# Eleven expert tiles for thirteen in a hybrid encoder layer: free blocks with register-addressed weights

## The chip, the core and the metric

The kernel runs on one core of a Trainium2 chip. The metric is device microseconds of one execution, the median of several runs. The profile shows one further execution; its stretches are named by microseconds from its first instruction. TensorE, VectorE, ScalarE, GpSimd and SyncE appear in it as PE, DVE, ACT, POOL and SP, and PEld is TensorE's load of stationary weights.

## What is computed

One layer for 512 tokens of width 1024, all float32: a latent attention and a neighbourhood attention side by side, an output projection, and then a mixture of experts, which is where the change lies. Cut to that part:

```python
p_g = softmax(h @ w_rg + b_rg); g_idx = top_k(p_g, 1)            # one of 4 groups
p_e = softmax(le[of that group]); e_idx = top_k(p_e, 2)           # two of its 4 experts
combine = one_hot(4 * g_idx + e_idx) * weights                    # (512, 16)
a, u = h @ w_gate[e], h @ w_up[e]                                 # 1024 -> 256, 16 experts
out = x + sum_e (silu(a) * u * combine[e]) @ w_down[e]            # 256 -> 1024
```

Each token goes to two of 16 experts, so there are 1024 rows to compute. With the kernel's numbering of the experts (places 0 to 15) the router gives on these inputs 46, 64, 53, 69, 48, 87, 59, 36, 44, 165, 62, 35, 56, 90, 76 and 34 rows to them.

## The kernel before

**Tiles and blocks.** The expert stage works in tiles of 128 rows, each of four blocks of 32 rows. A block has one expert: `gate_up(g)` (L1669) runs 8 k-steps of four 512-column products, one per block, each against its own expert's weights (the trace shows every float32 product as two, 64 in all); `hid_turns` (L1690) transposes the hidden rows; `down(g)` (L1696) shows as 32 products. `loads_of(g)` (L332) says which expert each block has. It is a table fixed when the kernel is built: every expert has 96 places (`CAP`), 16 experts fill 12 tiles, and one further tile, the thirteenth (g = 12, `LAST`), is given to the first expert that has more than 96 rows (its number is read from a register by SP alone, `expert`, L415). Only if more were needed would `passes` (L345) run further tiles, one after another. With the counts above one is enough: expert 9 has 69 rows beyond 96.

**How rows get there and back.** DVE works out a slot for each row (`ranks_out`, L1086). POOL scatters rows into a buffer in HBM, `slot_rows`, with indirect transfers, two per 128 tokens (`dispatch`, L604, `send`, L596). Rows beyond an expert's own places wait for the counts: PE sums them (`counted`, L1651), DVE works out the further tile (`extras_out`, L1211) and the slots (`slots_out`, L1232), and POOL sends them (`overflow`, L626). Each tile's rows come back to SBUF (`load_x` on ACT's queue, L861; the first three from SP), are transposed by PE (`x_turns`, L1657) and scaled by DVE (`x_read`, L1247). The result is scaled into one of two buffers `y_sb`, left half by ACT (`left_y`, L876), right half by DVE (`right_y`, L1272), and POOL adds it to the output with an indirect accumulating transfer (`add`, L634, issued at L638). Before `add(g)` POOL waits for `add(g - 2)` (`added`, L643); the thirteenth waits for the one before too.

**Order on the queues.** SP loads expert weights, 2048 KB gate and up (`load_gu`, L405) and 1024 KB down (`load_dn`, L409), into rings of six buffers each. Load n may start when the last tile that uses load n - 6 is through (L472 to L480). The wait stands in SP's program, so all that SP issues later stands behind it. On PE the order of the steady loop (L1722 to L1730) is: `gate_up(g)`, `down(g - 1)`, `x_turns(g + 2)`, `hid_turns(g)`. On DVE it is `hidden(g)`, `right_y(g - 1)`, `x_read(g + 2)`, `tile_tags(g + 2)`, `hidden_read(g)`.

The parts that set the order are these:

```python
for g in range(ITEMS):            # POOL, L649
    if g >= 2:
        added(g - 2)
    add(g)
    if g < 2:
        overflow(2 * g)
        overflow(2 * g + 1)
```

Of the kernel before, what the change touches and what calls it, by code (L numbers as in the profile page):

```python
# [6 lines left out]
P = 128  # L7
# [37 lines left out]
CAP, BLK = 96, 32  # L45
ITEMS = E * CAP // P
EARLY = P // BLK
EXTRA = EARLY + (TOP * SEQ - EARLY * (CAP - BLK + 1)) // (CAP + 1)
FAR = 1 << 20
RING = 6  # L50
# [8 lines left out]
NK = K_FLOOR + E  # L59

# [7 lines left out]
def build(nc, x, x_turned, cols_d, rows_d, rope_d, rpb_d, consts_d, w_in_lat, w_in_k, w_in_q, w_in_v, w_qb, w_kvb, w_out, w_r,  # L68
# [8 lines left out]
    with ctx:  # L77
# [56 lines left out]
        konst = at(89, NK)  # L134

        w_gu = [at(kb, KD, 2 * F) for kb in (16, 48, 120, 32, 64, 0)]
        w_dn = [at(kb, 2, D_MODEL) for kb in (80, 171, 195, 179, 187, 136)]
# [8 lines left out]
        x_end, x_start, x_tmp, x_adj = (at(92.5 + i / 16, E) for i in range(4))  # L146
        x_hit = at(153, EXTRA, E)
        tag_sb = at(153.75, TILES, 2)
        tag_row = at(153.9375, TILES, 1).bitcast(i32)
        x_prod = at(154.0625, T, TOP, E)  # L150
# [34 lines left out]
        x_expert = sm(EXTRA).bitcast(i32)  # L185
        counts = sm(E)
# [56 lines left out]
        s_wgu = [sem(f"w_gate_up_in{r}") for r in range(RING)]  # L243
        s_wdn = [sem(f"w_down_in{r}") for r in range(RING)]
# [4 lines left out]
        s_add = [sem(f"y{r}_added_to_out") for r in range(2)]  # L249
        s_wts, s_tag = sem("row_tags_ready"), sem("tile_tags_ready")  # L250
# [64 lines left out]

        LAST = ITEMS

        turned = [("h", 0)]
        for g in range(1, LAST + 1):
            turned += [("x", i, b) for i in ((1, 2, 3) if g == 1 else (g + 2,) if g + 2 <= LAST else ()) for b in range(2)]  # L320
            turned += [("h", g)]
# [10 lines left out]
        def loads_of(g):  # L332

            if g < 3:
                return ([0, 1, 2, 3], [0, 0, 1, 1], [2, 2, 3, 3])[g]
            return [(4 * g + b) // 3 if g < ITEMS else E + g - ITEMS for b in range(4)]

        def last_item(n):
            return max(g for g in range(TILES) if n in loads_of(g))

        def added_before(g):

            return 16 * (g // 2)
# [29 lines left out]
        def _(sp):  # L373
# [31 lines left out]
            def load_gu(n, e):  # L405
                sp.dma_start(w_gu[n % RING].rearrange("p (q k) f -> p q (k f)", q=4),
                             row(w_gu_d, e)).then_inc(s_wgu[n % RING], 16)

            def load_dn(n, e):  # L409
                sp.dma_start(w_dn[n % RING], row(w_dn_d, e)).then_inc(s_wdn[n % RING], 16)  # L410
# [4 lines left out]
            def expert(n):  # L415

                if n < E:
                    return n
# [75 lines left out]
            for g in range(LAST - 1, LAST + 1):  # L494
                sp.wait_ge(s_add[g % 2], added_before(g) + 16)

        @block.gpsimd
        def _(pool):
# [132 lines left out]

            pool.wait_ge(s_out, 16 * T)

            def add(g):  # L634
# [3 lines left out]
                nc.gpsimd.indirect_dma_start(  # L638
                    out=out_rows, out_offset=bass.IndirectOffsetOnAxis(ap=tag_row[:, g, 0:1], axis=0),
                    in_=y_sb[g % 2], in_offset=None,  # L640
                    bounds_check=SEQ - 1, oob_is_err=False, compute_op=ALU.add).then_inc(s_add[g % 2], 16)

            def added(g):  # L643

                pool.wait_ge(s_add[g % 2], added_before(g) + 16)

            for g in range(ITEMS):  # L649
                if g >= 2:  # L650
                    added(g - 2)
                add(g)
                if g < 2:
                    overflow(2 * g)
                    overflow(2 * g + 1)
            added(LAST - 2)
            added(LAST - 1)
            add(LAST)

            def extra_pool(g):  # L660
                added(g - 1)
# [6 lines left out]
        def _(act):  # L668
# [215 lines left out]
            for g in range(LAST + 1):  # L884
# [3 lines left out]
                if g == 0:  # L888
                    act.wait_ge(s_disp[1], 16 * TOP * 2)
                    load_x(3)  # L890
                if g + 4 <= LAST:
                    if g + 4 == LAST:
                        act.wait_ge(s_over, 16 * TOP * T)
                    load_x(g + 4)
                if 0 < g < LAST:
                    left_y(g - 1)
# [9 lines left out]
        def _(dve):  # L906
# [179 lines left out]
            def ranks_out(t):  # L1086
# [9 lines left out]
                nc.vector.tensor_scalar(over, KB_OF[t][:, 32:32 + E], CAP - 0.5, float(FAR), ALU.is_gt, ALU.mult).then_inc(s_cnt, 1)  # L1096
                dve.wait_ge(s_cnt, t + 1)
                link(nc.vector.tensor_tensor(early, early, slot, ALU.add))
                link(nc.vector.tensor_tensor(early, early, over, ALU.add))
# [110 lines left out]
            ranks_out(T - 1)  # L1210
            def extras_out():  # L1211

                dve.wait_ge(s_countr, 1)
# [605 lines left out]
```

## Time and profile before

| what | value |
|---|---|
| runs | 500.72, 502.74, 502.3 us; median 502.3 |
| the profiled execution | 502.5 us, its span 500.6 us |
| mean granted TensorE clock | 0.981 |
| TensorE busy | 464.3 us, 93% |
| DVE, ACT, POOL busy | 44%, 30%, 31% |
| DMA | 102.66 MB, 205 GB/s over the span |

The expert stage begins at about 327 us and lasts to the end. Busy PE time holds pipelined products, so it is the intervals between equal steps that tell a tile's cost. In a row of the timeline the columns are start, length, engine, line, operation, operands, count, and in brackets the idle time ahead and what ended it. In the rows of windows the DMA share is that of 16 engines; it can come out a little over 1.

### The profile page before, as it was taken

The numbers are of one execution on the slowest core, as the hardware profiler recorded it, in microseconds if no ns is written. First come the engines' busy times: TensorE is split into PE (matmuls) and PEld (weight loads), VectorE is DVE, ScalarE is ACT, GpSimd is POOL, SyncE is SP. The second block draws the span as 40 slices with busy tenths as digits, with TensorE's granted clock in tenths as the row PEclk, the third lists the DMA queues.
The fourth block names the chain that finished last, engine by engine and source line by source line (L and its number), as shares of the span: only waits on it lengthen the run. The fifth ranks groups of instructions, "written<-read, shape, count | busy, mean of one in ns | idle before, by whom it ended". The sixth has DMA issues, their size and how long they took to land.

```text
span 500.6 us, 7676 instructions
## 1 busy us (share of the span) xinstructions
PE 464.3 (93%) x2826; PEld 226.8 (45%) x2826; DVE 220.1 (44%) x696; ACT 147.8 (30%) x340; POOL 152.9 (31%) x163
## 2 busy tenths in 40 slices
PE   5999999989999999999999998896999999998982
PEld 2544544444555565554556555632333333342320
DVE  2133855515765545454555748655222222231310
ACT  1322513325455566453343523230001011000000
POOL 1150288878299920000000202220351111111121
PEclk9999999999999999999999989879999999999997
DMA  8999960005100000094010349799599999999531
GB/s 317 386 412 363 403 264 2 1 0 209 65 2 0 1 1 1 9 404 177 0 45 1 126 169 347 288 344 354 192 356 383 389 375 403 389 374 398 171 56 26
DMA packets 28873, 102.66 MB, mean 205 GB/s; under 512 B 3744, under 2 KB 5280, under 8 KB 28448
## 3 DMA queue, kind: packets, MB, share of 16 engines
q1 hardware_dynamic: 22640, 88.25, 45.7%
q0 software_dynamic: 4176, 8.42, 7.0%
q10 hardware_dynamic: 2016, 5.46, 2.8%
q8 instruction: 25, 0.41, 0.3%
q14 instruction: 16, 0.13, 0.1%
HBM read 79.50 MB, written 29.44 MB: 218 GB/s over the span
## 4 chain that ended last, share of the span: by engine, by line
PE 72%; DVE 8%; POOL 7%; DMA 6%; issue 5%; ACT 1%; POOLq 0%; SPq 0%; DVEq 0%
PE bank L1685 17%; PE bank L1346 14%; PE bank L1516 10%; PE bank L1709 8%; PE bank L1330 6%; PE bank L1418 5%; PE bank L1435 5%; POOL small L509 3%; DMA slot_rows<-arena,small 3%; DMA arena<-slot_rows 3%; PE bank L1666 2%; PE bank L1459 2%; DVE arena L987 1%; POOL arena L365 1%; DVE arena L989 1%
## 5 line engine op out<-in xcount | busy, mean ns | idle before, releaser
L1346 PE MATMUL bank<-arena 128*128 128x512 f32 (+1 forms) x256 | 111.1, 584 | 5.4 <-DVE arena L931 5.4
L1685 PE MATMUL bank<-arena 128*32 128x512 f32 x832 | 94.1, 603 | 2.7 <-DVE arena L1269 1.8
L1346 PEld LDWEIGHTS bank<-arena 128*128 128x128 f32 x256 | 48.2, 195 | 53.5 <-issue 53.1
L1330 PEld LDWEIGHTS bank<-arena 128*128 128x128 f32 (+1 forms) x356 | 42.9, 141 | 39.3 <-issue 32.3
L638 POOL DMA_INDIRECT out<-arena x13 | 20.2, 1550 | 130.6 <-DVE arena L1276 101.4
L1330 PE MATMUL bank<-arena 128*128 128x128 f32 (+1 forms) x356 | 51.4, 277 | 5.7 <-DVE arena L994 2.8
L1516 PE MATMUL bank<-arena 128*128 128x512 f32 x112 | 55.6, 620 | 0.6 <-issue 0.6
L1685 PEld LDWEIGHTS bank<-arena 128*32 128x32 f32 x832 | 26.7, 111 | 58.7 <-issue 56.7
L1709 PE MATMUL bank<-arena 128*32 128x512 f32 x416 | 47.1, 593 | 1.0 <-DVE arena L1269 1.0
L1003 DVE COPY arena<-bank 128x512 f32<-128x512 f32 (+2 forms) x64 | 35.8, 582 | 22.2 <-PE bank L1330 22.2
L874 ACT ACTIVATE arena<-bank 128x256 f32<-128x256 f32 x13 | 5.0, 385 | 126.1 <-PE bank L1685 126.1
L513 POOL TENSOR_SCALAR small<-small 128x1 f32<-128x1 f32 x16 | 3.6, 223 | 123.6 <-DVE small L1042 71.8
L1262 DVE TENSOR_TENSOR arena<-arena,bank 128x256 f32<-128x256 f32 x13 | 5.5, 421 | 74.2 <-ACT arena L874 74.2
L728 ACT ACTIVATE arena<-arena,small 128x512 f32<-128x512 f32 (+2 forms) x64 | 34.7, 590 | 3.7 <-DVE small L1011 3.6
L509 POOL TENSOR_TENSOR small<-small 128x24 f32<-128x24 f32 (+2 forms) x7 | 29.8, 4261 | 16.3 <-DVE small L982 9.3
L1128 DVE TENSOR_REDUCE small<-bank 128x1 f32<-128x512 f32 x32 | 22.1, 692 | 28.4 <-PE bank L1418 28.3
L1418 PE MATMUL bank<-arena 96*128 96x512 f32 x64 | 34.0, 615 | 0.0
L790 ACT ACTIVATE arena<-bank,small 128x512 f32<-128x512 f32 x32 | 22.0, 688 | 34.6 <-DVE small L1128 34.5
L1435 PE MATMUL bank<-arena 128*64 128x128 f32 x416 | 29.8, 280 | 1.6 <-DVE arena L1003 1.6
L1435 PEld LDWEIGHTS bank<-arena 128*64 128x64 f32 x416 | 22.1, 136 | 16.3 <-issue 14.6
L529 POOL TENSOR_TENSOR arena<-arena 128x512 f32<-128x512 f32 (+2 forms) x20 | 22.0, 1121 | 21.5 <-issue 13.7
L1516 PEld LDWEIGHTS bank<-arena 128*128 128x128 f32 x112 | 19.5, 194 | 18.7 <-issue 18.7
(176 smaller groups left out, 500.3 us busy)
## 6 DMA issues: line engine op xcount, KB each, us to landing
arena<-in_w_gu SPq DMA_DIRECT2D x17, 2048.0 KB, 23.8
arena<-in_w_dn SPq DMA_DIRECT2D x17, 1024.0 KB, 22.7
slot_rows<-arena SPq DMA_DIRECT2D x1, 11822.0 KB, 47.7
arena<-slot_rows ACTq DMA_DIRECT2D x10, 514.0 KB
arena<-in_w_out SPq DMA_DIRECT2D x2, 2048.0 KB, 8.2
arena<-in_x_turned SPq DMA_DIRECT2D x4, 512.0 KB, 8.1
arena<-in_x SPq DMA_DIRECT2D x4, 512.0 KB, 13.3
arena<-in_w_in_k SPq DMA_DIRECT2D x1, 2048.0 KB, 14.7
```

The costliest lines, as they stand in the source:

```text
L509: nc.gpsimd.tensor_tensor(v, v, mhalf[:, 0:n], ALU.pow).then_inc(s_root, 1)
L529: nc.gpsimd.tensor_tensor(dst, src, src, ALU.mult).then_inc(s_sqr, 1)
L728: nc.scalar.activation(probs, probs, ACT.Copy, scale=rsum[:, t % 2, u // MU, h:h + 1]).then_inc(s_ps, 1)
L1003: nc.vector.tensor_copy(PT[u % 2][:, 0:blocks, :], TPB[p % 2][:, 0:blocks * P].rearrange("p (a b) -> p a b", a=blocks))\
L1128: nc.vector.tensor_reduce(nmax[:, u % 2, u % H:u % H + 1], SB[u % 2][:, :], AX.X, ALU.max, negate=True).then_inc(s_mx, 1)
L1330: last = nc.tensor.transpose(TPB[p % 2][0:s.shape[-1], b * P:(b + 1) * P], s, ident)
L1346: last = nc.tensor.matmul(product_bank(i)[:, 0:width], hT[:, t, k, :], w[:, k, :], start=(k == 0), stop=(k == KD - 1))
L1418: nc.tensor.matmul(SB[u % 2][:, :], qT[:, h, t * P:(t + 1) * P], kT[:, h, :], start=True, stop=True).then_inc(s_S, 1)
L1435: last = nc.tensor.matmul(OB[t % 2][DV * j:DV * (j + 1), pair * P:(pair + 1) * P], v[:, first + b, h * DV:(h + 1) * DV], PT[j][:, b, :], s ...
L1516: last = nc.tensor.matmul(YB[b][:, :], src[:, k, :], w_o[half][:, k, b * 512:(b + 1) * 512], start=(k == 0), stop=(k == 3))
L1685: last = nc.tensor.matmul(GU[g % 2][BLK * b:BLK * (b + 1), :], xT[g % 2][:, k, BLK * b:BLK * (b + 1)], w_gu[n % RING][:, k, :], start=(k = ...
L1709: last = nc.tensor.matmul(YR[g % 2][half][BLK * b:BLK * (b + 1), :], hidT[g % 2][:, k, BLK * b:BLK * (b + 1)], w_dn[n % RING][:, k, half * ...
```

## The change

The layout of blocks becomes a table of 11 tiles. Most experts have two blocks of their own (64 rows), experts 14 and 15 four, and in tiles 3 to 9 the first block is free: DVE gives it, from the counts, to an expert whose weights are in SBUF at that time, and PE reads their place from a register, for gate/up and for down. Further tiles run only if rows are left, from none up (`EXTRA` is 15, `slot_rows` has 26 tiles for 23). The ring of gate/up weights has seven buffers, the seventh over `h2s`, the rows that POOL scatters; so SP waits for the last overflow transfer before that load, and ACT waits for it before it loads tiles 3, 4 and 5. All eight overflow transfers are issued ahead of the first add. Each add waits for the one before, and a tile with a free block is added in two transfers, one after the other: its first 32 rows, then the 128 with the first 32 out of range. `extras_out` and `slots_out` do more, and `places_out` is new.

```diff
-CAP, BLK = 96, 32
-ITEMS = E * CAP // P
+BLK = 32
+GU_RING, DN_RING = 7, 6
+FREE = -1
+LAYOUT = [[0, 1, 2, 3], [0, 1, 2, 3], [4, 4, 5, 5], [FREE, 6, 6, 7], [FREE, 7, 8, 8], [FREE, 9, 9, 10],
+          [FREE, 10, 11, 11], [FREE, 12, 12, 13], [FREE, 13, 13, 14], [FREE, 14, 14, 14], [15, 15, 15, 15]]
+ITEMS = len(LAYOUT)
+LAST_USE = [1, 1, 1, 3, 3, 4, 5, 5, 6, 8, 9, 9, 9, 9, 9, 10]
...
+EXTRA = 15
...
+GU_KB = (16, 48, 120, 32, 64, 0, 92.875)
...
-        LAST = ITEMS
-
-        turned = [("h", 0)]
+        LAST = ITEMS - 1
+
+        def turned_in(g):
+
+            return {1: (), 2: (3, 4)}.get(g, (g + 2,) if g + 2 <= LAST else ())
...
             with ExitStack() as more:
-                for i in range(1, EXTRA):
+                for i in range(EXTRA):
...
             load_dn(5, 5)
-            for g in range(LAST):
-                for n in range(RING, E + 1):
-                    if last_item(n - RING) == g - 1:
+            sp.wait_ge(s_over, 16 * TOP * T)
+            load_gu(6, 6)
+            for g in range(ITEMS):
+                for n in range(GU_RING, E):
+                    if LAST_USE[n - GU_RING] == g:
+                        sp.wait_ge(s_gu, g + 1)
+                        load_gu(n, n)
+                for n in range(DN_RING, E):
+                    if LAST_USE[n - DN_RING] == g - 1:
                         sp.wait_ge(s_dn, 2 * g)
-                        load_dn(n, expert(n))
-                for n in range(RING, E + 1):
-                    if last_item(n - RING) == g:
-                        sp.wait_ge(s_gu, g + 1)
-                        load_gu(n, expert(n))
+                        load_dn(n, n)
...
+            for t in range(T):
+                overflow(t)
             pool.wait_ge(s_out, 16 * T)
...
+                if loads_of(g)[0] == FREE:
+                    add_rows(g, tag_row[:, g, 0:1], BLK)
+                    pool.wait_ge(s_add[g % 2], added_before(g) + 16)
+                    add_rows(g, own_row[:, g - FREE_0, 0:1], P)
+                else:
+                    add_rows(g, tag_row[:, g, 0:1], P)
+
+            for g in range(LAST):
+                if g > 0:
+                    added(g - 1)
                 add(g)
...
-            for g in range(LAST + 1):
+            silu(0)
+            left_y(0)
+            silu(1)
+            act.wait_ge(s_over, 16 * TOP * T)
+            for g in (3, 4, 5):
+                load_x(g)
+            for g in range(2, LAST + 1):
...
                 for k in steps:
                     for b, n in enumerate(loads_of(g)):
+                        if n == FREE:
+                            w = arena[:, bass.ds(free_at[g][0] + k * 2 * F, 2 * F)]
+                        else:
+                            w = w_gu[n % GU_RING][:, k, :]
...
+            def free_places(g):
+
+                if g == FREE_0:
+                    pe.wait_ge(s_free, 1)
+                i = g - FREE_0
+                free_at[g] = [pe.value_load(v[0:1, i:i + 1], min_val=0, max_val=int(max(kbs) * KB))
+                              for v, kbs in ((gu_at, GU_KB), (dn_at, DN_KB))]
```

In the cut parts, `extras_out` becomes 50 small DVE instructions for 18 up to the point where it sets `s_most`, and the four behind that move into `extra_places_out`, after the first tiles' tags; `slots_out` becomes 18 for 10, most of them of 64 elements per partition; `places_out` adds 11 after the tags of tile 2. Every free tile adds one DVE instruction to its tags.

## Rows read from the trace of the kernel before

**Rows 1.** The page: PE's busy time, and the DMA row in 40 slices of 12.5 us.

```profile
PE 464.3 (93%) x2826; PEld 226.8 (45%) x2826; DVE 220.1 (44%) x696; ACT 147.8 (30%) x340; POOL 152.9 (31%) x163
...
DMA  8999960005100000094010349799599999999531
```

**Rows 2.** Timeline of PE, expert stage.

```profile
346.49 1.09 PE L1666 MATMUL bank<-arena 128*128 128x128 f32 x8 [3.04 <-DMA arena<-slot_rows]
...
357.19 7.07 PE L1685 MATMUL bank<-arena 128*32 128x512 f32 x64
...
368.87 7.07 PE L1685 MATMUL bank<-arena 128*32 128x512 f32 x64
...
452.57 7.07 PE L1685 MATMUL bank<-arena 128*32 128x512 f32 x64 [1.76 <-DVE arena L1269]
459.43 3.64 PE L1709 MATMUL bank<-arena 128*32 128x512 f32 x32
```

**Rows 3.** Windows: length, busy us of PE, PEld, DVE, ACT, POOL, clock, DMA share, GB/s.

```profile
325.00:330.00 5.00, 4.07 (x20) 2.05 (x23) 2.67 (x22) 4.12 (x13) 1.07 (x2) 0.50 1.00 324
...
350.00:355.00 5.00, 5.00 (x52) 1.56 (x48) 0.67 (x5) 0.00 (x0) 0.00 (x0) 1.00 0.33 105
...
360.00:465.00 105.00, 103.19 (x938) 37.42 (x934) 27.81 (x77) 9.65 (x18) 20.33 (x17) 1.00 1.03 383
```

**Rows 4.** Timeline of SP's queue.

```profile
338.75 0.51 SPq L410 DMA_DIRECT2D arena<-in_w_dn  x1
355.92 0.94 SPq L406 DMA_DIRECT2D arena<-in_w_gu  x2
```

**Rows 5.** DMA queues of 380 to 400 us: packets, MB, share of 16 engines.

```profile
q1 hardware_dynamic: 1513, 5.95, 73.3%
q0 software_dynamic: 527, 0.75, 16.8%
q10 hardware_dynamic: 288, 1.05, 12.9%
```

**Rows 6.** Timeline of DVE, routing work beside tile 0.

```profile
333.06 0.60 DVE L1216 SCALAR_TENSOR_TENSOR arena<-small,arena 128x16 f32<-128x16 f32 x3
...
333.90 0.15 DVE L1220 COPY arena<-arena 128x1 f32<-128x1 f32 x1
...
334.17 0.17 DVE L1220 COPY arena<-arena 128x2 f32<-128x2 f32 x1
...
338.38 0.42 DVE L1262 TENSOR_TENSOR arena<-arena,bank 128x256 f32<-128x256 f32 x1 [1.76 <-ACT arena L874]
...
340.08 0.22 DVE L1238 TENSOR_TENSOR arena<-arena 128x64 f32<-128x64 f32 x1
```

**Rows 7.** Timeline of POOL: two overflow transfers, the add of tile 6, the last add.

```profile
361.25 0.97 POOL L598 DMA_INDIRECT slot_rows<-arena,small  x1 [0.30 <-issue]
362.52 0.97 POOL L598 DMA_INDIRECT slot_rows<-arena,small  x1 [0.30 <-issue]
...
427.83 1.53 POOL L638 DMA_INDIRECT out<-arena  x1 [10.13 <-DVE arena L1276]
...
492.89 1.54 POOL L638 DMA_INDIRECT out<-arena  x1 [9.18 <-DVE arena L1276]
```

**Rows 8.** The chain that ended last: landings of two scatters, the last add's release.

```profile
311.54 9.40 DMA slot_rows<-arena,small
...
332.43 5.44 DMA slot_rows<-arena,small
...
491.95 0.02 issue
```

**Rows 9.** The software queue in 432.3 to 436.6 us: packets, MB, share.

```profile
q0 software_dynamic: 144, 0.31, 37.0%
```

**Rows 10.** SP's last wait, for the last adds: length in ns and time.

```profile
L495 SPq EVENT_SEMAPHORE  x1: 28/28/28, 499.2 to 499.2; - x1
```

**Rows 11.** Register work of SP's one register-addressed gate/up load: length in ns.

```profile
L406 SPq FUSED_REGOPS  x1: 48/48/48, 447.9 to 447.9; - x1
```

More of the change, by code:

```diff
@@ L58 @@
 K_FLOOR = K_LOW + E
-NK = K_FLOOR + E
+K_CAP = K_FLOOR + E
+K_FROM = K_CAP + E
+K_END = K_FROM + E
+K_MOST = K_END + E
+K_GU = K_MOST + E
+K_DN = K_GU + E
+K_LEAST = K_DN + E
+K_OWN = K_LEAST + FREES
+NK = K_OWN + 1
+GU_KB = (16, 48, 120, 32, 64, 0, 92.875)
+DN_KB = (80, 171, 195, 179, 187, 136)
 TILES = ITEMS + EXTRA
@@ L637, in add @@
                 pool.wait_ge(s_tag, g + 1)
[L638 to L651, printed above, removed]
-                add(g)
[L653 to L657, printed above, removed]
+                if loads_of(g)[0] == FREE:
[7 more added lines that the diff above has]
+                    added(g - 1)
+                add(g)
             add(LAST)
             def extra_pool(g):
+                added(g - 2)
                 added(g - 1)
@@ L1210, in _, with table, running @@
             ranks_out(T - 1)
+            def table(k):
+                return konst[:, k:k + E]
+            def running(a, b, op):
+                for shift in (1, 2, 4, 8):
+                    nc.vector.tensor_copy(b[:, 0:shift], a[:, 0:shift])
+                    link(nc.vector.tensor_tensor(b[:, shift:E], a[:, shift:E], a[:, 0:E - shift], op))
+                    a, b = b, a
             def extras_out():
                 dve.wait_ge(s_countr, 1)
-                link(nc.vector.tensor_scalar(x_tmp, counts, float(CAP), None, ALU.is_gt))
@@ L1215, in extras_out @@
-                for bound in range(CAP + P, SEQ, P):
-                    link(nc.vector.scalar_tensor_tensor(x_tmp, counts, float(bound), x_tmp, ALU.is_gt, ALU.add))
-                a, b = x_start, x_end
-                link(nc.vector.tensor_copy(a, x_tmp))
-                for shift in (1, 2, 4, 8):
-                    nc.vector.tensor_copy(b[:, 0:shift], a[:, 0:shift])
-                    link(nc.vector.tensor_tensor(b[:, shift:E], a[:, shift:E], a[:, 0:E - shift], ALU.add))
-                    a, b = b, a
+                link(nc.vector.tensor_tensor(beyond, counts, table(K_CAP), ALU.subtract))
@@ new lines, in extras_out @@
+                link(nc.vector.tensor_scalar(wanted, beyond, 1.0, None, ALU.is_gt))
+                for bound in range(BLK, max(FREE_MOST) * BLK, BLK):
+                    link(nc.vector.scalar_tensor_tensor(wanted, beyond, bound + 1.0, wanted, ALU.is_gt, ALU.add))
+                link(nc.vector.tensor_tensor(wanted, wanted, table(K_MOST), ALU.min))
+                link(nc.vector.tensor_copy(sum_a, wanted))
+                running(sum_a, sum_b, ALU.add)
+                link(nc.vector.tensor_tensor(sum_a, sum_a, wanted, ALU.subtract))
@@ new lines, in extras_out @@
+                link(nc.vector.tensor_tensor(max_a, table(K_FROM), sum_a, ALU.subtract))
+                running(max_a, max_b, ALU.max)
+                link(nc.vector.tensor_tensor(f_start, max_a, sum_a, ALU.add))
+                link(nc.vector.tensor_tensor(f_blocks, table(K_END), f_start, ALU.subtract))
+                link(nc.vector.scalar_tensor_tensor(f_blocks, f_blocks, 0.0, wanted, ALU.max, ALU.min))
+                nc.vector.tensor_scalar(f_row, f_start, float(P), None, ALU.mult)
+                nc.vector.tensor_scalar(f_rows, f_blocks, float(BLK), None, ALU.mult)
@@ L1223, in extras_out @@
+                link(nc.vector.scalar_tensor_tensor(x_rows, f_blocks, -float(BLK), beyond, ALU.mult, ALU.add))
+                link(nc.vector.tensor_scalar(x_tmp, x_rows, 1.0, None, ALU.is_gt))
+                for bound in range(P, SEQ, P):
+                    link(nc.vector.scalar_tensor_tensor(x_tmp, x_rows, bound + 1.0, x_tmp, ALU.is_gt, ALU.add))
+                link(nc.vector.tensor_copy(x_start, x_tmp))
+                running(x_start, x_end, ALU.add)
                 link(nc.vector.tensor_copy(x_end, x_start))
@@ L1301, in _ @@
                 tile_tags(g)
+            places_out()
+            extra_places_out()
             for g in range(1, LAST + 1):
@@ L1307, in _ @@
                     right_y(g - 1)
-                if g + 2 <= LAST:
-                    x_read(g + 2)
-                    tile_tags(g + 2)
+                for i in turned_in(g):
+                    x_read(i)
+                    tile_tags(i)
                 hidden_read(g)
```

182 lines of the change are left out of this document (120 added, 62 removed).

## The prediction

> **What bounds the kernel now.** I read the page first: PE is busy 93% of the span, and in its last third the DMA row stands at nine tenths too [rows 1]. So two resources are near their limit in the expert stage, and taking a tile away from one of them need not move the end. The timeline of PE gives the price of a tile: gate/up of tile 2 starts at 357.19 us, that of tile 3 at 368.87, so 11.68 us, and the same from tile to tile up to the ninth [rows 2]. The one break in the pattern is ahead of tile 10, at 452.57, 1.8 us. The windows show the DMA engines full from 360 to 465 us (share 1.03, 383 GB/s), but two thirds idle just ahead of that, 0.33 in 350 to 355 us [rows 3]. The timeline of SP's queue says why: its load at 338.75 is the last that is free to go, and the next waits for tile 1's products, at 355.92 [rows 4]. So PE sets the pace and the DMA keeps up with nothing in hand.
>
> The price of each kind of transfer comes from the queues of 380 to 400 us [rows 5]. SP's queue moved 5.95 MB in 73.3% of 20 us, 406 GB/s: 5.2 us for a gate/up load of 2.1 MB, 2.6 us for a down load. ACT's queue moved two row tiles in 12.9%: 1.3 us each. Two adds took 16.8%: 1.7 us each, in occupied engine time; their delay is another matter, below.
>
> **Two tiles less.** The counts fit the new table: experts 3, 5, 9 and 13 have 5, 23, 101 and 26 rows beyond 64, which want 1, 1, 4 and 1 free blocks, seven in all, and their windows (tile 3; 3 or 4; 5 to 8; up to 9) hold them. No further tile runs. On PE alone: 2 x 11.68 = 23.4 us less, a span of 477.2.
>
> **The routing work on DVE.** The steps of 16 columns come every 0.20 us, those in pairs every 0.14 (333.90 to 334.17) [rows 6]. The new `extras_out` has 50 steps for 18, 24 of them in pairs: 26 x 0.20 + 24 x 0.14 = 8.6 us. It starts two steps ahead of 333.06 as before, so it ends near 341.4. `hidden(0)` ran at 338.38 [rows 6] and goes 3 us later, and `down(0)` with it, which so ends at about 346.3. Its cover is the wait for tile 1's rows, which PE turned at 346.49 after 3.04 us idle [rows 2]; without that cover it would cost 3 us. `slots_out` has 18 steps of 64 columns, 0.22 us long [rows 6] and 0.25 with the link between two; from 342.7 it ends at about 347. `x_read(1)` then starts near 348, 0.7 us late, which I leave in the rounding. `places_out` (11 steps, 3 us) and the longer tags lie beside tile 1's products. The larger zero fill (26 tiles for 23) and constants lie in stretches where the DMA row is 0 or 1 [rows 1]: nothing.
>
> **The load behind the overflow.** Eight overflow transfers now go together from 347.2, one each 1.27 us [rows 7], the last is issued by 357.4. From there to landing a scatter took 5.44 and 9.40 us with the engines full [rows 8]; here they are empty, so I take 4.5, with 3 and 8 as ends: 362. SP may load expert 6 only then, and ACT the rows of tiles 3 to 5. Behind SP's wait stands every later weight load, those of experts 7, 8 and 9 first, which were free since 356. Tile 3 needs 6 and 7: 2 x 5.2, with three row tiles (3.9) and an add (1.7) between them, and about 2 us until the last byte counts: 380. Tile 3 began at 368.87 before, so 11 us of the 23 go back.
>
> **Then the transfers bound it.** Until `down(7)` can run, the experts' loads up to down 13 must land: from 362 us 10 gate/up and 8 down loads (72.8 us), 8 row tiles (10.4) and 5 adds (8.5): 454. What PE still has then equals what it had in the kernel before at `down(9)`: from 459.43 to the end, 500.6, 41.2 us [rows 2]. So this limit gives a span of 495, 5.4 less than now, if the adds stay hidden.
>
> **The adds.** Here I find the new bound. The add that POOL starts at 427.83 [rows 7] has its 144 packets in 432.3 to 436.6 us [rows 9]: 8.8 us from start to landing while the queue of weights is full. The last one starts at 492.89 [rows 7] and SP sees it at 499.2 [rows 10]: 6.3 us with nothing beside it, of which 2.1 are ahead of the packets if these take the same 4.3. So far no one waits for either, since an add waits only for the one two before. Now each waits for its predecessor, and tiles 3 to 9 have two in a row. Release to start is 0.94 us (491.95 to 492.89) [rows 7, 8]. The 32-row transfer is not in the trace: its packets start as late (4.5 us full, 2.1 empty) and take between a quarter of 4.3 us and all of it, so 5.6 to 8.8 us full, 3.2 to 6.3 empty. I take 5.9 and 3.5, near the lower ends, as it has a quarter of the rows. A free tile then costs POOL 5.9 + 0.9 + 8.8 + 0.9 = 16.5 us under load and 3.5 + 0.9 + 6.3 + 0.9 = 11.6 us without, against the 11.68 of PE.
>
> The chain in order: gate/up of tile 3 at 380.5, of tile 4 at 392.2, `down(3)` ends at 402.7, its two halves are scaled at 403.5, POOL starts at 404.4. Three cycles under load put the add of tile 6 at 454, where the weights run out. Tiles 6 to 9 take 11.6 us each, with 3 us more for the last two down loads that still come: tile 10's add starts at 503, lands at 509.5, and 1.4 us later the program ends (499.2 to 500.6): 511. Behind POOL's waits stand `left_y` and `right_y`, which need the buffer back, so DVE's `right_y(g - 1)` holds `hidden_read(g)` and PE runs at most three tiles ahead; that costs nothing more as long as the adds are the slower chain.
>
> The Trainium skill, DMA: Bandwidth & Descriptors, section "Anatomy of one DMA — SWDGE (gpsimd) path", fits one such transfer as 2.0 us plus its bytes at 436 GB/s. By that rule a 128-row add would take 3.2 us and a 32-row one 2.3, and the pair with its releases 7.3 us, hidden under any tile. The row shows 6.3 us for the 128 rows, and 8.8 under load, so I go by the rows.
>
> **Registers on PE.** A quarter of a free tile's 96 products, 24, are addressed by a register. SP's one such load shows 48 ns of register work [rows 11]: 1.2 us a tile if PE's sequencer isn't ahead, some 2 with the two register loads; nothing if it is. I take nothing, since PE waits for weights or for the adds in these tiles; as upper end 7 x 2 = 14 us. After waits the granted clock was 0.50 in 325 to 330 us [rows 3], the lower of the two levels; after the gap of some 12 us ahead of tile 3 I expect the same for a few microseconds. On its own that adds 3 us to tile 3, in the upper end.
>
> **Sum.** 500.6 - 23.4 + 11 + 7 (transfers) gives the 495 of the hidden case, and + 16 from the adds gives 511. The profiled execution was 1.9 us over its span (502.5 for 500.6) and 0.2 over the median of the runs, so the time is 513 us, 2.1% over 502.3. A change of under 0.5% can hardly be told from none.
>
> **Rivals.**
> 1. *The adds stay hidden, the transfers bound it.* Place: tiles 3 to 9. It holds if a pair of adds takes under about 13 us with loads beside it. For it: fewer adds crowd the queue. Against: 8.8 us for one alone [rows 7, 9]. Time: 495 + 1.9 = 497, faster by 1%. Chance 0.20.
> 2. *PE stays the bound.* The overflow lands by 356, as the loads went before, and the free blocks don't hold weights back: 477.2 + 1.9 = 479, or up to 490 with half of the stall. Against: eight transfers can't be issued before 357, and the engines were full with six buffers. Chance 0.09.
> 3. *Registers and clock.* PE pays 2 us in each free tile and runs part of it at the lower clock, in a chain with the adds' waits: 513 + 10 to 513 + 16, so 523 to 529. Chance 0.11.
> 4. *A further tile runs after all*, serial, with its own loads: at least 20 us, 530 or more. The counts speak against it. Chance 0.03.
> The forecast has 0.57, with 505 to 521 as its own range (32-row transfer at its two ends, overflow landing 3 us either way).
>
> **How the numbers follow.** Slower by over 0.5% (above 504.8): the forecast but for 0.05 of it, and rivals 3 and 4: 0.66. Faster (below 499.8): rival 2 and 0.13 of rival 1, 0.22. The rest, 0.12, is within. The range must reach rival 1 and the lower half of rival 3: 494 to 524.
>
> **What would show it.** In the trace of the changed kernel: 11 groups of 64 gate/up products; idle PE ahead of the third of them in tile 3, to about 380 us; SP's first load after 338 at about 362; POOL's adds in tiles 3 to 9 as pairs, 15 to 17 us from pair to pair under load, back to back, with POOL waiting for DMA rather than for DVE L1276; DVE's and ACT's scaling waiting for DMA; SP's queue drained well before 470. I am wrong if POOL still waits for DVE between tiles, if PE has no gap ahead of tile 3, or if a pair takes under 12 us.

## The result, and the profile after

| kernel | median | ratio to before | span of the profiled run |
|---|---|---|---|
| before, measured beside it | 501.92 us (4 runs) | | 500.6 us |
| changed | 534.55 us (533.29 to 536.09, 4 runs) | 1.0654, interval 1.0615 to 1.0692 | 534.3 us |

The changed kernel is 6.5% slower. The prediction had the sign (slower, 0.66) but not the size: 513 with 494 to 524. What happened is the forecast's chain and rival 4 behind it: a twelfth tile ran.

In the changed kernel the products of gate/up stand at L1799, those of down at L1827, the turning of rows at L1776, the adds at L679, SP's loads at L448 and L452, the overflow's scatters at L640 and the scaling that releases an add at L1382. The page, with PE, the clock row and the DMA row in slices of 13.4 us, answers to [rows 1]:

```profile
PE 469.0 (88%) x2720; PEld 225.9 (42%) x2720; DVE 226.3 (42%) x747; ACT 146.7 (27%) x338; POOL 160.8 (30%) x169
...
PEclk9999999999999999999999895799898998999577
DMA  8999950005000000930107499919999999543810
```

PE has 106 products fewer. Two tiles would be twice 106 (`thr7` below, with both gone, has 2614), so only one tile has gone. At the end of the DMA row stands an "8" that the kernel before did not have. The timeline of PE (start, length, engine, line, operation, count, idle time ahead and what ended it) answers to [rows 2]:

```profile
379.78 8.77 PE L1799 MATMUL bank<-arena 128*32 x64 [2.50 <-DMA arena<-in_w_gu]
...
403.34 5.34 PE L1827 MATMUL bank<-arena 128*32 x32 [3.10 <-DMA arena<-in_w_dn]
...
454.71 7.07 PE L1799 MATMUL bank<-arena 128*32 x64
...
466.39 7.07 PE L1799 MATMUL bank<-arena 128*32 x64
...
489.62 3.64 PE L1827 MATMUL bank<-arena 128*32 128x512 f32 x32 [0.52 <-DVE arena L1375]
507.18 1.97 PE L1776 MATMUL bank<-arena 128*128 128x128 f32 x8 [13.92 <-DMA arena<-slot_rows]
...
509.93 8.89 PE L1799 MATMUL bank<-arena 128*32 128x512 f32 x64 [0.78 <-DVE arena L1359]
```

Tile 3 starts at 379.78, where 380 was forecast. Two neighbouring free tiles, 454.71 and 466.39, are 11.68 us apart, so products addressed by a register cost nothing. `down(10)`, the last planned step, starts at 489.62; then PE is idle for 13.92 us and a further tile begins. The timeline of SP's queue answers to [rows 4]:

```profile
338.32 0.43 SPq L452 DMA_DIRECT2D arena<-in_w_dn  x1
360.42 9.32 SPq L448 DMA_DIRECT2D arena<-in_w_gu  x4
...
494.06 0.41 SPq L448 DMA_DIRECT2D arena<-in_w_gu  x1
```

SP's first late load goes at 360.42 (forecast 362), behind the overflow. The weights and the rows of the further tile are issued only when `down(10)` is through. The chain that ended last shows the rows landing 12 us later:

```profile
495.15 11.98 DMA arena<-slot_rows
```

Last, the timeline of POOL, which answers to [rows 7]:

```profile
357.58 0.97 POOL L640 DMA_INDIRECT slot_rows<-arena,small  x1 [0.30 <-issue]
...
410.45 1.33 POOL L679 DMA_INDIRECT out<-arena  x1 [15.17 <-DVE arena L1382]
...
428.79 1.33 POOL L679 DMA_INDIRECT out<-arena  x1 [10.12 <-DMA out<-arena,small]
...
445.38 1.33 POOL L679 DMA_INDIRECT out<-arena  x1 [8.34 <-DMA out<-arena,small]
...
461.85 1.33 POOL L679 DMA_INDIRECT out<-arena  x1 [8.09 <-DMA out<-arena,small]
...
472.64 1.33 POOL L679 DMA_INDIRECT out<-arena  x1 [5.04 <-DMA out<-arena,small]
...
504.82 1.54 POOL L679 DMA_INDIRECT out<-arena,small  x1 [5.91 <-DMA out<-arena]
506.67 1.54 POOL L679 DMA_INDIRECT out<-arena  x1 [0.30 <-issue]
526.16 1.54 POOL L679 DMA_INDIRECT out<-arena  x1 [17.95 <-DVE arena L1382]
```

The last scatter starts at 357.58, near the 357.4 forecast. In tiles 4 to 9 POOL waits for DMA, not for DVE as in [rows 7], but for two adds (435.50, released by DVE, and 486.09, by ACT). From pair to pair it is 18.3, 16.6 and 16.5 us with the weights' queue full, where 16.5 was forecast, and 10.8, 13.5 and 11.5 without, where 11.6 was forecast. So nearly all of the forecast stands in this trace, and a tile behind it.

### The profile page after: what moved, and what is told of

Its sections match the earlier page's. It is cut to its first block, busy times and chain, and to the rows that moved or that the text cites. A ratio compares the mean times of both kernels' runs of the same rounds, so it can differ in the third digit from the quotient of the medians.

```text
span 534.3 us, 7638 instructions
## 1 busy us (share of the span) xinstructions
PE 469.0 (88%) x2720; PEld 225.9 (42%) x2720; DVE 226.3 (42%) x747; ACT 146.7 (27%) x338; POOL 160.8 (30%) x169
## 4 chain that ended last, share of the span: by engine, by line
PE 63%; DMA 15%; DVE 9%; POOL 6%; issue 4%; ACT 1%; SPq 0%; POOLq 0%; DVEq 0%
PE bank L1456 13%; PE bank L1799 11%; PE bank L1626 10%; DMA arena<-in_w_gu 7%; PE bank L1827 6%; PE bank L1440 5%; PE bank L1545 5%; PE bank L1528 5%; DMA arena<-in_w_dn 5%; POOL small L551 3%; DMA arena<-slot_rows 2%; PE bank L1569 2%; PE bank L1636 1%; PE bank L1652 1%; PE bank L1776 1%
## 5 line engine op out<-in xcount | busy, mean ns | idle before, releaser
L1799 PE MATMUL bank<-arena 128*32 128x512 f32 (+1 forms) x768 | 95.1, 631 | 7.1 <-DMA arena<-in_w_gu 4.6
L1456 PEld LDWEIGHTS bank<-arena 128*128 128x128 f32 x256 | 48.4, 196 | 54.2 <-issue 53.8
L1827 PE MATMUL bank<-arena 128*32 128x512 f32 (+1 forms) x384 | 48.5, 649 | 9.9 <-DMA arena<-in_w_dn 8.4
L1799 PEld LDWEIGHTS bank<-arena 128*32 128x32 f32 x768 | 25.1, 115 | 66.7 <-issue 65.4
L679 POOL DMA_INDIRECT out<-arena x12 | 17.1, 1424 | 110.4 <-DVE arena L1382 64.9
L640 POOL DMA_INDIRECT slot_rows<-arena,small x16 | 16.0, 997 | 51.7 <-DVE small L1154 32.6
L1827 PEld LDWEIGHTS bank<-arena 128*32 128x32 f32 x384 | 14.0, 118 | 41.3 <-issue 38.5
L1382 DVE TENSOR_SCALAR arena<-bank,arena 128x512 f32<-128x512 f32 x12 | 9.0, 751 | 52.9 <-PE bank L1827 38.2
```

The source lines that it names most:

```text
L1456: last = nc.tensor.matmul(product_bank(i)[:, 0:width], hT[:, t, k, :], w[:, k, :], start=(k == 0), stop=(k == KD - 1))
L1799: last = nc.tensor.matmul(GU[g % 2][BLK * b:BLK * (b + 1), :], xT[g % 2][:, k, BLK * b:BLK * (b + 1)], w, start=(k == 0), stop=(k == KD - 1))
L1827: last = nc.tensor.matmul(YR[g % 2][half][BLK * b:BLK * (b + 1), :], hidT[g % 2][:, k, BLK * b:BLK * (b + 1)], w, start=(k == 0), stop=(k ...
```

## Why a tile was left over

The expert stage places the first 256 tokens before all counts are known. So that the next tokens' rows start behind each early block, `pads` (L1141 here, L1091 before) raises the count of an expert of tile 0 to the 32 rows of its block when the first 256 tokens brought fewer. In the kernel's own order of tokens these bring 30, 26, 29 and 57 rows to experts 0 to 3 (counted from the reference's router), so 2, 6, 3 and 0 places stay empty. Expert 1 has 64 rows, which looked like an exact fit in two blocks; with six empty places it needs 70. Its weights are used last in tile 1, where no block is free. Six rows are over, and the kernel runs a whole tile for them.

The kernel before has the same pads. They cost it nothing, since 96 places hold 70.

## The experiments

The runs fall into four groups, each on one chip with the kernel before beside it (medians 502.9, 503.18, 503.42 and 503.57 us, in the order below); each ratio is within its group. The number that DVE compares to decide on a further tile is half more than the rows left, since `K_CAP` holds 32 rows per block less a half: 6.5 for six rows.

### thr6 and thr7: without the further tile

`thr6` (one run) and `thr7` raise the bound from which a further tile runs. `thr7` so leaves six of the 1024 rows uncomputed, and with them the further tile.

```diff
-                link(nc.vector.tensor_scalar(x_tmp, x_rows, 1.0, None, ALU.is_gt))
+                link(nc.vector.tensor_scalar(x_tmp, x_rows, 7.0, None, ALU.is_gt))   # thr6: 6.0
```

> The changed kernel, but a further tile is asked for only where an expert has more than 6 rows left over, instead of more than 0.5. Theory P (the padding of tile 0 pushes expert 1 to 70 places of 64, 6 rows over, and that is what calls the twelfth tile): 6.5 counts as over, the tile runs, 534 us as for the changed kernel. Rival Q (many rows are left over, because the free blocks don't reach the experts they were meant for): 534 us here as well, and again 534 with a bound of 7. Rival R (only one to five rows over): no further tile, about 514.

> The same with more than 7 rows as the bound; no further tile if 6 rows are all that is left over, and those 6 of 1024 rows stay out of the result. Theory P: the rest of the trace is unchanged, the last add starts near 506.5 and lands 6.3 us later, so a span of 514 and a time of 515 to 516, ratio 1.027 to the kernel before. Rival Q: 534 as before.

`thr6`: 535.67 us, so the tile still ran. `thr7`: 511.02 us, ratio 1.0144 (1.0102 to 1.0185), and no further tile. The compared number is over 6 and not over 7, as the 6.5 that the pads give: six rows are left, and no more. The tile costs 0.051 by the ratios, some 25 us; the spans, 534.3 and 509.8, say 24.5. `thr7` is the case that the forecast spoke of, and its time lies 2 us beside the 513; it is 4 us below the 515 to 516 expected of this run, since the last add starts at 502.55 and not near 506.5. Its chain that ended last, in order of time:

```profile
422.12 26.32 DMA arena<-in_w_dn
...
468.26 5.37 DMA out<-arena,small
...
474.43 3.59 DMA out<-arena
...
478.79 6.17 DMA out<-arena,small
...
485.75 3.30 DMA out<-arena
...
489.81 6.43 DMA out<-arena,small
...
497.04 2.90 DMA out<-arena
```

Up to 449 us it waits for weights, and from 468 on it is adds one after another, the 32 rows (2.9 to 3.6 us) and the 128 (5.4 to 6.4).

### one and lag: without the pairs, without the wait

Both stand on `thr7` and leave out the free blocks' rows: tiles 3 to 9 have one add. `lag` also waits, from tile 3 on, only for the add two before, as the kernel before does, and ahead of the last add for both that are still out.

```diff
-            return 16 * (2 if loads_of(g)[0] == FREE else 1)
+            return 16
...
-                    add_rows(g, tag_row[:, g, 0:1], BLK)
-                    pool.wait_ge(s_add[g % 2], added_before(g) + 16)
                     add_rows(g, own_row[:, g - FREE_0, 0:1], P)
...
-                    added(g - 1)
+                    added(g - (1 if g < 3 else 2))        # lag alone
...
+            added(LAST - 2)                               # lag alone
+            added(LAST - 1)                               # lag alone
```

> As the one with the bound of 7, but in tiles 3 to 9 only the second of the two adds is issued, so the rows of the free blocks are left out of the result; each add still waits for the one before. Theory A (from tile 3 on the serial pairs of adds set the end): 8 to 12 us less than with both, 503 to 507. Rival B (the weights' transfers set the end, the adds are hidden behind them): within 2 us of the one with both adds.

> As the last one, and from tile 3 on an add waits only for the one two before, as in the kernel before. Theory A: once there is one add per tile it takes 9.7 us with the release, under the tile's 11.68, so the wait costs under 2 us more; the transfers are the bound then, a time of 497 to 503. Rival C (the wait itself costs much even with one add): 5 us or more below the last one.

`one`: 503.78 us (1.0007, 0.9983 to 1.0031). `lag`: 504.25 us (1.0027, 0.9999 to 1.0054), 1 us above its expected range. So the second add of each pair costs 7.2 us (511.02 to 503.78), and waiting for the one before instead of the one two before costs nothing. And with the adds out of the way the kernel is still no faster than before, though it runs two tiles less. Why is seen in `lag`. Timeline of PE:

```profile
411.79 9.75 PE L1799 MATMUL bank<-arena 128*32 x64 [5.72 <-DMA arena<-in_w_gu]
...
449.39 6.39 PE L1827 MATMUL bank<-arena 128*32 x32 [4.22 <-DMA arena<-in_w_dn]
...
463.85 3.62 PE L1827 MATMUL bank<-arena 128*32 x32
```

The chain that ended last, between these:

```profile
361.44 18.54 DMA arena<-in_w_gu
...
388.77 22.79 DMA arena<-in_w_gu
...
425.05 24.11 DMA arena<-in_w_dn
```

And the windows (length, busy us of PE, PEld, DVE, ACT, POOL, clock, DMA share, GB/s):

```profile
405.00:425.00 20.00, 14.28 (x107) 4.28 (x106) 3.14 (x10) 1.07 (x2) 1.54 (x1) 0.83 1.02 392
...
445.00:450.00 5.00, 0.78 (x8) 0.38 (x8) 0.42 (x1) 0.38 (x1) 0.00 (x0) 0.80 1.02 382
```

From 361 to 450 us three loads stand on the chain, each landing 18 to 24 us after its release, with the engines full (share 1.02 to 1.03 in every window from 365 to 450). Over the two stretches shown, each with a wait in it, the granted clock is 0.83 and 0.80, a mix of its two levels of 1.2 and 2.4 GHz, and the steps behind the waits are longer: 9.75 us for a gate/up that else takes 7.07, 6.39 for a down that else takes 3.62.

### half and laghalf: a shorter overflow

The first 256 tokens have no row beyond their places, so the first four of the eight overflow transfers carry nothing. `half` is `thr7` without them, `laghalf` is `lag` without them.

```diff
-            sp.wait_ge(s_over, 16 * TOP * T)      # and the same on ACT
+            sp.wait_ge(s_over, 16 * TOP * 2)
...
-            for t in range(T):
+            for t in range(2, T):
                 overflow(t)
```

> As the one with the bound of 7 (both adds), but only the last four overflow transfers are issued, those of tokens 256 to 511, and SP and ACT wait for these; the first four carry no row on these inputs. Theory S (the loads behind the overflow hold up tile 3, one for one): SP's first late load at 355 instead of 360, tile 3's products 5 us earlier, and as everything behind it shifts, 4 to 6 us less in all, 505 to 507. Rival T (the order of the weights' transfers is the bound, not their start): 2 us or less.

> The same with one add per tile and the wait for the one two before. Theory S: 4 to 6 us under the 504.3 of that kernel with all eight overflow transfers, 498 to 500. Rival T: 502 or more. If nearly all of the gap of 5 us in tile 1's products goes too, the burst of transfers on POOL is what made it.

`half`: 504.62 us (1.0024, 0.9997 to 1.0051), 6.4 below `thr7`. `laghalf`: 497.86 us (0.9889, 0.9854 to 0.9924), 6.4 below `lag`. In `half`, SP's queue and then PE:

```profile
353.31 9.98 SPq L448 DMA_DIRECT2D arena<-in_w_gu  x4
```

```profile
373.38 8.77 PE L1799 MATMUL bank<-arena 128*32 x64 [3.13 <-DMA arena<-in_w_gu]
```

In `thr7` the same two steps stand at 361.27 and 380.67 us. The first late load goes 8.0 us earlier, tile 3 starts 7.3 earlier, and the medians move by 6.4, with pairs and without (6.0 and 6.9 by the ratios, as the kernels compared are of different groups). Both times lie just below their expected ranges. But the shorter overflow is not all that differs: in the traces of `thr7` and `lag` tile 1's products stall for some 5 us (last section), in those of `half` and `laghalf` they don't. In `thr7` tile 3 waits last for DVE L1375 (1.83 us), on a chain that goes back through that stall. How much of the 6.4 us is the stall's is not shown. The pair in the next experiment is free of it.

### lay and layhalf: a place for expert 1's six rows

`lay` computes all rows. It gives expert 1 a third block of its own, in tile 2, and keeps 11 tiles and seven free blocks. `layhalf` is `lay` with the four empty overflow transfers left out.

```diff
-LAYOUT = [[0, 1, 2, 3], [0, 1, 2, 3], [4, 4, 5, 5], [FREE, 6, 6, 7], [FREE, 7, 8, 8], [FREE, 9, 9, 10],
-          [FREE, 10, 11, 11], [FREE, 12, 12, 13], [FREE, 13, 13, 14], [FREE, 14, 14, 14], [15, 15, 15, 15]]
+LAYOUT = [[0, 1, 2, 3], [0, 2, 3, 1], [1, 4, 4, 4], [FREE, 5, 5, 6], [FREE, 6, 7, 7], [FREE, 8, 8, 9],
+          [FREE, 9, 10, 10], [FREE, 11, 11, 12], [FREE, 12, 13, 13], [FREE, 14, 14, 14], [15, 15, 15, 15]]
...
-LAST_USE = [1, 1, 1, 3, 3, 4, 5, 5, 6, 8, 9, 9, 9, 9, 9, 10]
+LAST_USE = [1, 2, 1, 3, 3, 4, 5, 5, 6, 8, 9, 9, 9, 9, 9, 10]
```

> The changed kernel with another table of blocks and nothing else: expert 1 gets a third block of its own (tile 1 is 0, 2, 3, 1 and tile 2 is 1, 4, 4, 4), expert 5 moves to tile 3, and all experts from 6 on move back by one or two blocks. All rows are computed. Theory P: no further tile, as 70 places fit in 96. Tile 3 needs only the weights of expert 6, not 7, so it starts at about 375 instead of 380. The pairs of adds still end last: 506 to 511. Rival Q: a further tile still runs, 530 or more.

> That table with the last four overflow transfers alone. All rows are computed on these inputs. By theory S and the table together the weights come 5 us sooner: 502 to 507, so at best level with the kernel before, as the pairs of adds remain. If it comes out under 500, the adds have slack.

`lay`: 506.54 us (1.0074, 1.0041 to 1.0107), 28 us less than the changed kernel for a change of two tables. `layhalf`: 502.32 us (0.9984, 0.996 to 1.0008). Both are within what was expected. They are of one group, and neither trace has the stall: the first late load goes at 358.83 and at 355.31, and 3.5 us there are worth 4.2 at the end (4.5 by the ratios). So with the order of the loads as it is, the expert stage has hardly any slack behind the overflow. The chain that ended last of `lay` prices the adds:

```profile
440.25 6.77 DMA out<-arena
...
447.79 9.00 DMA out<-arena,small
...
457.58 3.49 DMA out<-arena
...
461.84 6.59 DMA out<-arena,small
```

From POOL's start to landing 32 rows take 6.8 us under load and 3.4 to 3.7 without, 128 rows 9.0 and 5.7 to 6.6. The 6.8 is a high one: in the chains of `half`, `layhalf` and `order` 32 rows under load take 5.9 to 6.2 us.

### order and orderlag: loads in order of need

Both compute on `lay`'s table. Expert 6's gate and up go into the buffer that tile 1 frees, expert 7's over `h2s`, and SP issues the loads in the order in which PE needs them. `orderlag` also has one add per free tile (the free blocks' rows left out) and, from tile 4 on, waits for the one two before (in `lag` from tile 3 on).

```diff
+def place(n):
+    return {6: 0, 7: 6}.get(n, n % GU_RING)
...
-            sp.wait_ge(s_over, 16 * TOP * T)
+            sp.wait_ge(s_gu, 2)
             load_gu(6, 6)
-            for g in range(ITEMS):
...
+            sp.wait_ge(s_over, 16 * TOP * T)
+            load_gu(7, 7)
+            sp.wait_ge(s_dn, 4)
+            load_dn(6, 6)
+            sp.wait_ge(s_gu, 3)
+            load_gu(8, 8)
+            load_gu(9, 9)
+            load_dn(8, 8)
...
```

> The table with three own blocks for expert 1, and the weights of experts 6 and 7 change places: 6 goes into the buffer that tile 1 frees, 7 into the one over the scattered rows, and SP issues the loads in the order in which they are needed. All rows are computed, all eight overflow transfers and both adds are there. Theory S with A: the first late load goes at 356, no wait for weights in tile 3 or for the down load in tile 3, so the first pair of adds starts at about 395 instead of 405.5. Behind it the pairs take 16.5 us under load and 11.6 without, 91.7 us from tile 3 to tile 10 in the kernel with that table, up to 98 now as more of them run beside loads: a span of 494 to 501, a time of 496 to 503. Rival T: nothing gained over the 506.5 of the table alone.

> The same with one add in tiles 3 to 9 (the rows of the free blocks stay out of the result) and, from tile 4 on, the wait for the add two before. What the pairs of adds still cost: theory A says 5 to 12 us, so 486 to 494, with PE close to its pace of 11.68 us a tile. If it comes within 3 us of the one with the pairs, the transfers are the bound there too.

`order`: 505.39 us (1.0048, 1.002 to 1.0076), 2 us above the expected range; its interval and that of `lay` overlap, so the rival "nothing gained" is not ruled out. `orderlag`: 493.01 us (0.9827, 0.9783 to 0.9871). In `order` the rows of the next tiles arrive late, then the last step of PE:

```profile
370.01 1.09 PE L1792 MATMUL bank<-arena 128*128 128x128 f32 x8 [2.22 <-DMA arena<-slot_rows]
372.61 1.97 PE L1792 MATMUL bank<-arena 128*128 128x128 f32 x8 [1.51 <-DMA arena<-slot_rows]
...
480.38 5.34 PE L1843 MATMUL bank<-arena 128*32 128x512 f32 x32 [0.52 <-DVE arena L1391]
```

and the adds of POOL:

```profile
400.79 1.33 POOL L695 DMA_INDIRECT out<-arena  x1 [10.18 <-DVE arena L1398]
...
495.84 1.54 POOL L695 DMA_INDIRECT out<-arena  x1 [0.30 <-issue]
```

PE is through at 485.7, the last add starts ten microseconds later: here the chain of adds is the bound, 95 us from 400.79 to 495.84, and the pairs, with the wait for the add before, cost 12.4 us (505.39 to 493.01).

Why so little came of the earlier loads is in the same trace. Expert 6's load goes at 356.02, as meant, but the last overflow scatter now lands beside it. The chain that ended last has it as

```profile
355.55 7.62 DMA slot_rows<-arena,small
```

In `lay` the last scatter starts at 355.70 and ACT loads the next tiles' rows 3.1 us later; here it is 7.6 us. Tile 3 has its weights but waits for its rows and starts at 374.94, later than `lay`'s 372.13. What is gained comes behind it: `down(3)`, which waits 6.33 us for its weights in `lay`, has them here, so the first pair of adds starts at 400.79 (405.55 in `lay`, 395 expected). In `orderlag` the rows come later still:

```profile
374.44 1.97 PE L1792 MATMUL bank<-arena 128*128 128x128 f32 x8 [5.89 <-DMA arena<-slot_rows]
...
380.50 8.26 PE L1815 MATMUL bank<-arena 128*32 x64
```

### alt and layalt: a shorter chain of adds

In tiles 4, 6 and 8 the 128-row add goes first, without waiting for the one of the tile before; then come both waits and the 32 rows. The 32 rows of the next tile follow them. So of four transfers per two tiles only three stand in a row. Neighbouring tiles' adds of 128 rows are then in flight together, as they are in the kernel before, where `add(g)` waits for `add(g - 2)` alone; no more freedom than that was taken. `alt` has this on `order`, `layalt` on `lay`; both compute all rows.

```diff
-                if loads_of(g)[0] == FREE:
+                if loads_of(g)[0] == FREE and g % 2:
                     add_rows(g, tag_row[:, g, 0:1], BLK)
...
+                elif loads_of(g)[0] == FREE:
+                    add_rows(g, own_row[:, g - FREE_0, 0:1], P)
+                    added(g - 1)
+                    pool.wait_ge(s_add[g % 2], added_before(g) + 16)
+                    add_rows(g, tag_row[:, g, 0:1], BLK)
...
-                if g > 0:
+                if g in (1, 2) or g % 2:
                     added(g - 1)
```

> The last kernel with both adds, but in tiles 4, 6 and 8 the own rows go first, without a wait for the own rows of the tile before (their experts are of different groups, so no token is in both), and the free block's rows go last. Two adds of 128 rows then run side by side in every second tile, and the chain of a pair of tiles has three landings to wait for and a release in place of four: under load about 6.8 + 9.7 + 1.9 + 6.8 = 25 us for 33, so 12.6 a tile, near PE's 11.68. Theory A: of the 12.4 us that the pairs cost in that kernel 9 to 11 go, 494 to 497, faster than both kernels. If the adds' landings slow each other down by as much, 500 or more.

> The table with three own blocks for expert 1 (506.5 us), the loads in the order of the changed kernel, and the same alternating adds. Theory A: the transfers are the next bound, between tile 3's later start and the free adds, 499 to 502. If it is as low as the one with the ordered loads, that order is worth nothing.

`alt`: 499.63 us (0.9927, 0.9899 to 0.9954), `layalt`: 499.5 us (0.9946, 0.9915 to 0.9977). Both beat the kernel before, by 0.5 to 0.7% by the ratios, and the changed kernel by 35 us. That is a small gain over the kernel before, but both intervals end below 1. `layalt` is within its expected range, `alt` came out 3 us above its own. Between these two the order of the loads is worth nothing measurable. But in the profiled run of `alt` its early start was missing: SP's first late load waits for tile 1's products, these stalled (last section), and it went at 363.31 and not at 356.02 as in `order`:

```profile
363.31 0.94 SPq L454 DMA_DIRECT2D arena<-in_w_gu  x2
```

Later two down loads hold PE, until 424.44 and 454.56. How much of the 3 us is due to the stall is not shown. The timeline of POOL in `alt`:

```profile
408.66 1.54 POOL L695 DMA_INDIRECT out<-arena,small  x1 [5.41 <-DMA out<-arena]
413.47 1.54 POOL L695 DMA_INDIRECT out<-arena,small  x1 [3.27 <-issue]
423.63 1.33 POOL L695 DMA_INDIRECT out<-arena  x1 [8.63 <-DMA out<-arena,small]
```

The second 128 rows start 4.8 us after the first and don't wait for their landing. Not tried: one add for both kinds of rows. A token may stand in the free block and in an own block of the same tile, which is why the change adds them apart.

## Why the prediction was wrong, step by step

**Two tiles less: the step that failed.** "The counts fit the new table ... No further tile runs." I took the rows that the router gives and compared them with the places. The kernel compares rows and pads, and for expert 1 that is 70 against 64. Rival 4 named the outcome and got 0.03, because I took the fit of 64 in 64 for a certainty. Its price was right as a bound ("at least 20 us, 530 or more"): 24.5 us by the spans, 534.55 in all. A fit without a place to spare should have sent me to every line that changes the count.

**The routing work on DVE** ended at 347.57 (347 forecast), but its cover was thinner than I had it: `down(0)` ended at 348.55, not 346.3, and tile 1's products started at 350.63, 1.8 us later than before and not 0.7. That cost nothing by itself, as tile 3 waited for its weights all the same.

**The load behind the overflow: right in its two times.** 362 forecast, 360.42 measured; tile 3 at 380, measured 379.78. Between the last scatter's start and SP's load lie only 2.8 us; I had 4.5, with 3 as the lower end. The "about 2 us until the last byte counts" in the sum for tile 3 have no row behind them, and no run shows them apart. What four overflow transfers fewer are worth is 4.2 us by `lay` and `layhalf`; the 6.4 of `half` may have the stall in it.

**Transfers and adds: the sum right in part by luck, its split wrong.** I had 495 for the span with hidden adds, and 16 us for the adds. The runs give 502.3 (`one`) and 503.5 (`lag`), and 7.2 us. So the transfers cost 7 to 9 us more than I gave them and the adds 9 less. In the hidden case I had asked when all loads up to down 13 are in, 454 us, and let `down(7)` start there. In `lag` an earlier step binds: `down(6)` waits for its own weights until 449.39, takes 6.39 us at the lower clock and is followed by a gate/up, so `down(7)` starts at 463.85, ten later. The lower clock after a wait for weights stood in my upper end only, for tile 3 alone; on `lag`'s chain it is worth 2.7 and 2.8 us at the two steps shown above.

The chain of adds came out near 511 because errors cancel. In `thr7` the first pair starts at 411.0, not 404.4, since `down(3)` waits for weights too: 6.6 late. Three pairs under load take 53.1 us (411.00 to 464.06), not 49.5. But from there to the last add it is 38.5 us (to 502.55), not 49: the pairs without load take 10.4 to 11.3 us, the 3 us that I had added for the last loads don't show, and the last add waits for no other. I had read the loop over `range(LAST)` as if it held the last tile, but `add(LAST)` stands behind it without the wait. The changed kernel's row shows it too: 504.82 and 506.67, 0.30 us idle between them. I had 7.2 us for that step, and it takes 1.85.

**The price of the small transfer** was taken as 5.9 us under load and 3.5 without; the chains show 5.9 to 6.8 and mostly 2.9 to 3.9. That of 128 rows was 8.8 and 6.3, and is 8.9 to 11.0 and mostly 5.4 to 6.8. The Trainium skill's fit (DMA: Bandwidth & Descriptors, section "Anatomy of one DMA — SWDGE (gpsimd) path") would have been 2.3 and 3.2 us, pairs hidden and 497 in all; going by the rows was right. `order` against `orderlag` measures the pairs and their waits at 12.4 us where the adds are the bound.

**Registers on PE: right.** A free tile still takes 11.68 us.

**Rivals.** 1 fell twice: the pairs are not hidden, and even hidden the time is 503.8 and not 497. 2 fell: SP could not load before 360. 3 fell in its registers; its lower clock is there, worth up to 3 us a step. 4 happened.

## What the change is worth, in order

| what is done | time | ratio |
|---|---|---|
| changed kernel | 534.55 us | 1.065 |
| the further tile gone (`lay`, all rows) | 506.54 us | 1.007 |
| and the adds alternating (`layalt`, all rows) | 499.5 us | 0.995 |
| `order` without pairs (rows left out) | 493.01 us | 0.983 |

The last row is a bound, not a kernel that could be used. Of the 23.4 us that two tiles are worth on PE, some 10 are left in it (503.42 to 493.01), and some 4 in the best kernels that compute all rows. Where the other 13 go in `orderlag` its trace shows: tile 3 starts at 380.50, where the kernel before has it at 368.87, so 11.6 us are lost ahead of it, 7.7 of them in waits for rows, which may be loaded only behind the overflow. From there to tile 9 it loses another 4.5 us against 11.68 a tile.

## What to carry to other kernels

When a change cuts spare places, count what the code counts, paddings and rounding among them, and treat an exact fit as a warning. Where a resource idles before a burst and is full in it, the start of the burst can set the end nearly one for one; look for the wait that holds its first transfer, and for what that transfer will slow down when it goes earlier. Take for the end the first step that waits for its own data, not the sum of all loads. A transfer of a quarter of the rows still costs more than half of what the whole one does once each waits for the last (5.9 to 6.8 us against 9.0 under load, 3.5 against 6), so a chain of small dependent transfers has to be priced by its latency beside the load that it will meet.

## What was not expected of the hardware

**A stall inside tile 1's products.** 64 products that take 7.07 us in a row took about 12 in some profiled runs, with gaps that the trace puts down to no wait. The timeline of PE in the changed kernel:

```profile
350.63 5.77 PE L1799 MATMUL bank<-arena 128*32 128x512 f32 x49 [0.18 <-issue]
357.19 2.48 PE L1799 MATMUL bank<-arena 128*32 128x512 f32 x6 [0.80 <-issue]
360.05 2.48 PE L1799 MATMUL bank<-arena 128*32 128x512 f32 x9 [0.38 <-issue]
```

and in `lay`:

```profile
349.19 7.07 PE L1799 MATMUL bank<-arena 128*32 128x512 f32 x64 [0.18 <-DVE arena L1359]
```

`thr6`, `thr7`, `one`, `alt` and `layalt` have the gaps too, `half`, `laghalf`, `layhalf`, `order` and `orderlag` don't. `lag` belongs to the first: its records show no gap, but ACT gets the products only at 361.45, 12.2 us after their start. Eight overflow transfers stand beside it in `lay` and `order` as well, so these alone aren't the cause. It stays open. Each kernel has only one traced run, so how often the stall comes is not known; it matters wherever a load waits for tile 1's products.

**Empty transfers are not free.** A scatter with no row in range holds POOL for 1.27 us like a full one, and four of them, taken away, moved the end by 4.2 us in `layhalf`.

**The software queue is slow beside a full hardware queue.** Its adds of 32 rows take nearly twice as long beside the weights (5.9 to 6.8 against 3.5 us), those of 128 rows half as long again (9.0 against 5.7 to 6.6). So do the scatters: from the last one's start to what waits for it are 2.8 us in the changed kernel and 3.1 in `lay`, but 7.6 in `order` and 8.0 in `orderlag`, where a weight load is issued within a microsecond of it. Getting one transfer out earlier made the next wait longer.
